# A two-layer hybrid trunk on one core: layer 0's lower convolutions and gates moved in the step order, and the mLSTM's key sums and squares rearranged

## The reference, cut to what matters

```python
# layer 0, recurrence
xc = causal_dwconv(xa, ...)                    # 4 taps, 8 tiles of 128 channels
r = sigmoid(block_diag(xc, wa) + ba)           # per tile: gates r and i
i = sigmoid(block_diag(xc, wx) + bx)
log_a = -8 * r * softplus(-lam)
b = sqrt(-expm1(2 * log_a)) * (i * xc)
h = scan(exp(log_a), b); ya = h * gelu(ga)
# layer 1, mLSTM, for each head
C_new = decay * C + sum_s kw_s v_s^T           # 512 x 512, for 8 samples and the prompt
n_new = decay * n + sum_s kw_s                 # the key sums
h = num / max(|den|, exp(-m))
h = h * rsqrt(mean(h * h) + eps)               # the mean of squares over a head's 512 rows
```

## Time and profile before

| | |
|---|---|
| median of three runs | 1156.18 us |
| the profiled execution's own time | 1151.86 us |
| its span in the trace | 1149.9 us |
| PE busy | 1084.2 us (94%) |
| DVE busy | 660.5 us (57%) |
| ACT busy | 543.3 us (47%) |
| GpSimd busy | 155.0 us (13%) |
| DMA | 260.97 MB, mean 227 GB/s |
| chain that ended last | PE 82%, DVE 10%, ACT 4%, DMA 2%, issue 1% |

### The profile page before, as it was taken

How to read it: one execution, slowest core, us unless ns; L and a number is a source line. 1 busy time by engine, 2 the same in 40 slices (tenths; PEclk the granted TensorE clock), 3 DMA queues, 4 the chain that set the end, 5 groups by cost and what they waited for, 6 DMA issues and landing times.

```text
span 1149.9 us, 21693 instructions
## 1 busy us (share of the span) xinstructions
PE 1084.2 (94%) x8497; PEld 949.2 (83%) x8497; DVE 660.5 (57%) x958; ACT 543.3 (47%) x885; POOL 155.0 (13%) x204
## 2 busy tenths in 40 slices
PE   4998999889999999999999999999999999999995
PEld 4987777668989999999999865555547989999995
DVE  4559584632376444335997546667686376544333
ACT  5332544532466553434575254554643456553431
POOL 5133000000104220001400410100000104220000
PEclk9998999899999999999999999999999999999998
DMA  9697797999534444443743039898999434444431
GB/s 337 229 331 273 275 378 289 351 346 385 170 115 167 165 163 166 166 164 126 271 151 129 22 105 389 308 393 297 395 340 398 166 127 165 165 164 165 166 128 41
DMA packets 92264, 260.97 MB, mean 227 GB/s; under 512 B 8836, under 2 KB 9860, under 8 KB 91800
## 3 DMA queue, kind: packets, MB, share of 16 engines
q1 hardware_dynamic: 91320, 257.92, 62.5%
q0 software_dynamic: 432, 1.29, 0.4%
q10 hardware_dynamic: 432, 0.65, 0.2%
HBM read 218.10 MB, written 41.73 MB: 226 GB/s over the span
## 4 chain that ended last, share of the span: by engine, by line
PE 82%; DVE 10%; ACT 4%; DMA 2%; issue 1%; SPq 0%; DVEq 0%; ACTq 0%
PE ps L2000 20%; PE ps L2001 19%; PE ps L2002 19%; PE ps L2484 2%; PE ps L2457 2%; PE ps L2112 2%; DVE w_lo L1200 2%; PE ps L2355 2%; PE ps L2193 1%; PE ps L2487 1%; PE ps L2399 1%; PE ps L2362 1%; DVE rstd L1230 1%; PE ps L2094 1%; PE ps L2064 1%
## 5 line engine op out<-in xcount | busy, mean ns | idle before, releaser
L1200 DVE TENSOR_TENSOR w_lo<-w_raw,w_hi 128x1024 fp32r<-128x1024 f32 x232 | 284.7, 1234 | 215.0 <-ACT w_hi L696 214.3
L696 ACT ACTIVATE w_hi<-w_raw 128x1024 fp32r<-128x1024 f32 x232 | 242.1, 1054 | 213.8 <-PE ps L2002 184.1
L2000 PE MATMUL ps<-xin_hi,w_hi 128*128 128x288 f32 x1016 | 307.8, 303 | 20.0 <-DVE w_lo L1200 19.9
L2001 PE MATMUL ps<-xin_lo,w_hi 128*128 128x288 f32 x1016 | 303.7, 299 | 0.0
L2002 PE MATMUL ps<-xin_hi,w_lo 128*128 128x288 f32 x1016 | 303.5, 299 | 0.0
L2000 PEld LDWEIGHTS ps<-xin_hi,w_hi 128*128 128x128 f32 x1016 | 194.7, 192 | 32.2 <-DVE w_lo L1200 21.1
L2001 PEld LDWEIGHTS ps<-xin_lo,w_hi 128*128 128x128 f32 x1016 | 193.6, 191 | 0.8 <-issue 0.2
L2002 PEld LDWEIGHTS ps<-xin_hi,w_lo 128*128 128x128 f32 x1016 | 193.4, 190 | 0.0
L2001 PE MATMUL ps<-hid_lo,w_hi 128*128 128x288 f32 x512 | 151.6, 296 | 0.0
L2002 PE MATMUL ps<-hid_hi,w_lo 128*128 128x288 f32 x512 | 151.3, 295 | 0.0
L2000 PE MATMUL ps<-hid_hi,w_hi 128*128 128x288 f32 x512 | 151.2, 295 | 0.0
(11 more groups left out here) (401 smaller groups left out, 1679.9 us busy)
## 6 DMA issues: line engine op xcount, KB each, us to landing
w_raw<-in_weights SPq DMA_DIRECT2D x232, 512.0 KB, 3.3
cring<-in_C SPq DMA_DIRECT2D x64, 512.0 KB, 6.3
out_Cs<-cring SPq DMA_DIRECT2D x64, 512.0 KB, 6.7
kv_a<-in_kv SPq DMA_DIRECT2D x52, 448.0 KB, 5.9
kv_b<-in_kv SPq DMA_DIRECT2D x52, 448.0 KB, 6.2
kv_w<-in_kv SPq DMA_DIRECT2D x24, 448.0 KB, 7.7
out_Cp<-cring SPq DMA_DIRECT2D x8, 512.0 KB, 5.9
x<-in_x SPq DMA_DIRECT2D x1, 1152.0 KB, 7.6
```

Of the source, the lines that this page charges most:

```text
L696: act.activation(w_hi[:, l % UM], w_raw[:, l % W_SLOTS], ACT.Copy).then_inc(hi_ready, 1)
L1200: dve.tensor_tensor(w_lo[:, l % W_SLOTS], w_raw[:, l % W_SLOTS], w_hi[:, l % UM], ALU.subtract).then_inc(lo_ready, 1)
L2000: pe.matmul(out, w_hi[:, j, ws], hi, start=start and kk == 0, stop=False)
L2001: pe.matmul(out, w_hi[:, j, ws], lo, start=False, stop=False)
```

## The change

In layer 0 the lower convolutions move from DVE's turns 18 to 21 to 22 to 25, the upper ones from 28, 30, 32, 33 to 30, 32, 34, 35. The gates are made in pairs, r and i of one tile together, on PE from step 23 (from 21 before) and on ACT from 25 (from 23 before). `decays(0)`, `input_roots(0)`, `input_scale(0)`, `recurrence(0)` and `gated(0)` come two turns later, `branch_gelu(0)` one later, `sample_scale(0)` two earlier. In the mLSTM the key sums swap operands: the selector (now padded to 128 columns) is the stationary operand and the keys the moving one, so the sums come out as rows, with n0 and its result laid out as rows too (`nrows`, one load and one more store). GpSimd adds the four squared tiles before one matmul of ones. The core of the diff:

```diff
-AB_USES = (["qs", "q0", "ks", "k0"] + [f"r{m}" for m in range(4)] + [f"i{m}" for m in range(4)]
-           + [f"r{m}" for m in range(4, 8)] + [f"i{m}" for m in range(4, 8)])
+AB_USES = ["qs", "q0", "ks", "k0"] + [f"{g}{m}" for m in range(MT) for g in "ri"]
...
# ACT, layer 0
-                if 23 <= g < 27:
-                    for m in range(2):
-                        gates((g - 23) // 2, 2 * ((g - 23) % 2) + m)
-                if g == 26:
-                    decays(0)
+                if 25 <= g < 25 + HM:
+                    gates(0, g - 25)
+                    gates(1, g - 25)
                 if g == 27:
                     sample_exp(0)
                 if g == 28:
+                    decays(0)
+                if g == 30:
                     input_roots(0)
-                if g == 30:
+                if g == 31:
                     branch_gelu(0)
...
# DVE, layer 0
-                if 18 <= g < 18 + HM:
-                    conv(g - 18)
+                if 22 <= g < 22 + HM:
+                    conv(g - 22)
...
-                if g == 27:
+                if g == 28:
+                    sample_scale(0)
+                if g == 29:
                     input_scale(0)
-                if g == 29:
+                if g == 31:
                     recurrence(0)
-                if g == 30:
-                    sample_scale(0)
-                if g == 31:
+                if g == 33:
                     gated(0)
-                if g in (28, 30, 32, 33):
-                    conv(HM + (28, 30, 32, 33).index(g))
+                if g in (30, 32, 34, 35):
+                    conv(HM + (30, 32, 34, 35).index(g))
...
# PE, layer 0
-                if 21 <= g < 25:
-                    for m in range(2):
-                        lru_gate((g - 21) // 2, 2 * ((g - 21) % 2) + m)
+                if 23 <= g < 23 + HM:
+                    lru_gate(0, g - 23)
+                    lru_gate(1, g - 23)
...
-                if 33 <= g < 37:
-                    for m in range(2):
-                        lru_gate((g - 33) // 2, HM + 2 * ((g - 33) % 2) + m)
+                if 33 <= g < 33 + HM:
+                    lru_gate(0, HM + g - 33)
+                    lru_gate(1, HM + g - 33)
...
# DVE, mLSTM
-                decay = bc[:, h % 2, R_DECAY:R_DECAY + NB]
-                pn = staged_v(h, "n")[:, 0:ET * (NB + 2)].rearrange("p (e b) -> p e b", b=NB + 2)
-                kn = pack_n[:, h * ET:(h + 1) * ET]
-                order.mark(dve.tensor_copy(kn[:, :, 0:1], pn[:, :, NB:NB + 1]))
-                order.after(dve.tensor_tensor(kn[:, :, 1:], n0_of(h).rearrange("p (e b) -> p e b", b=NB),
-                                              decay.unsqueeze(1).to_broadcast([P, ET, NB]), ALU.mult))
-                dve.tensor_tensor(kn[:, :, 1:], kn[:, :, 1:], pn[:, :, 0:NB], ALU.add).then_inc(stage_read_v, 1)
+                own = slice(N_S, N_S + NB)
+                pn = staged_v(h, "n")
+                if h == 0:
+                    dve.wait_ge(n0_in, 16)
+                dve.scalar_tensor_tensor(nrows[own, h], nrows[own, h], dcol[own, h:h + 1], pn[own], ALU.mult, ALU.add)
+                dve.tensor_copy(nrows[N_P:N_P + 1, h], pn[N_P:N_P + 1]).then_inc(stage_read_v, 1)
...
# GpSimd, mLSTM
-            for h in range(1, NH):
-                if h >= 2:
-                    pool.wait_ge(stage_full, use(h - 2, "vs") + 1)
-                head_diagonals(h)
+            def row_sums(h):
+
+                pool.wait_ge(h_sq, h + 1)
+                order.after(pool.tensor_tensor(qf[:, 0:2, 0:SEQ], qf[:, 0:2, 0:SEQ], qf[:, 2:4, 0:SEQ], ALU.add))
+                pool.tensor_tensor(qf[:, 0, 0:SEQ], qf[:, 0, 0:SEQ], qf[:, 1, 0:SEQ], ALU.add).then_inc(h_sum, 1)
+
+            for h in range(NH):
+                if h + 1 < NH:
+                    if h >= 1:
+                        pool.wait_ge(stage_full, use(h - 1, "vs") + 1)
+                    head_diagonals(h + 1)
+                row_sums(h)
...
# PE, mLSTM
-            def key_sums(h, tiles):
-
-                out = staged(h, "n") if 0 in tiles else ps[:, 6 + use(h, "n") % 2]
-                for e in tiles:
-                    c0 = (NB + 2) * e
-                    es = slice(P * e, P * e + P)
-                    for tt in range(2):
-                        pe.matmul(out[:, c0 + NB:c0 + NB + 1], ktok[:, tt, es], tokg[:, tt, NH + h:NH + h + 1],
-                                  start=tt == 0, stop=tt == 1)
-                    last = pe.matmul(out[:, c0:c0 + NB], kst[:, h % 2, es], seln, start=True, stop=True)
-                if ET - 1 in tiles:
-                    last.then_inc(stage_full, 1)
+            def key_sums(h):
+
+                out = staged(h, "n")
+                pe.matmul(out, seln, kst[:, h % 2], start=True, stop=False, skip_group_check=True)
+                for tt in range(2):
+                    last = pe.matmul(out[N_P:N_P + 1], tokg[:, tt, NH + h:NH + h + 1], ktok[:, tt],
+                                     start=False, stop=tt == 1, skip_group_check=True)
+                last.then_inc(stage_full, 1)
...
-                pe.wait_ge(h_sq, h + 1)
+                pe.wait_ge(h_sum, h + 1)
                 out = staged(h, "mean")
-                for e in range(ET):
-                    last = pe.matmul(out[:, 0:SEQ], ones, qf[:, e, 0:SEQ], start=e == 0, stop=e == ET - 1)
-                last.then_inc(stage_full, 1)
+                pe.matmul(out[:, 0:SEQ], ones, qf[:, 0, 0:SEQ], start=True, stop=True).then_inc(stage_full, 1)
...
                     if b == 1:
-                        key_sums(h, (0, 1))
+                        key_sums(h)
                     if b == 2:
                         row_squares(h)
                     if b in (3, 4):
                         outer(h, NB, b - 3)
                     outer(h, b, 0)
-                    if b == 1:
-                        key_sums(h, (2, 3))
```

More of the change, by code:

```diff
@@ L269, in program @@
         stri, o = at("stri", o, NS, parts=NS)
-        sel3, o = at("sel3", o, 2, NB, parts=3 * NS)
-        seln, o = at("seln", o, NB, dt=F32R, parts=3 * NS)
+        seln, _ = at("seln", o + 4 * NB, P, dt=F32R, parts=3 * NS)
+        sel3, o = at("sel3", o, NB + P, parts=3 * NS)
         gsml, o = at("gsml", o, 2 + NB, parts=NH)
@@ L468, in program @@
         h_sq = sem("h_sq")
+        h_sum = sem("h_sum")
+        n0_in = sem("n0_in")
         hs_psum = sem("hs_psum")
@@ L865, in _ @@
                     branch_gelu(1)
-                if 35 <= g < 39:
-                    for m in range(2):
-                        gates((g - 35) // 2, HM + 2 * ((g - 35) % 2) + m)
+                if 35 <= g < 35 + HM:
+                    gates(0, HM + g - 35)
+                    gates(1, HM + g - 35)
                 if g == 38:
@@ L1058, in _ @@
             act.activation(w3, ps[0:3 * NS, 5, 6 * NH:7 * NH], ACT.Copy, scale=DH ** -0.5)
-            act.activation(seln, sel3[:, 1], ACT.Copy).then_inc(gcol_taken, 1)
+            act.activation(dcol[N_S:N_S + NB], ps[N_S:N_S + NB, 5, 7 * NH:8 * NH], ACT.Copy)
+            act.activation(seln, sel3[:, NB:], ACT.Copy).then_inc(gcol_taken, 1)
             act.wait_ge(gcol_taken, 1)
@@ L1099, in own_values @@
                     act.wait_ge(c_mm, item(ho, bo, 1) + 1)
-                act.activation(vb[:, n % 2], vst[:, h % 2], ACT.Copy, scale=sel3[:, 0, b:b + 1]).then_inc(vb_ready, 1)
+                act.activation(vb[:, n % 2], vst[:, h % 2], ACT.Copy, scale=sel3[:, b:b + 1]).then_inc(vb_ready, 1)
             def sample_roots(c):
@@ L2324, in gate_columns @@
                 pe.transpose(ps[0:NS, 5, 5 * NH:6 * NH], rows[:, R_ENS:R_ENS + NS], four)
+                pe.matmul(ps[N_S:N_S + NB, 5, 7 * NH:8 * NH], rows[:, R_DECAY:R_DECAY + NB], four, start=True, stop=True,
+                          skip_group_check=True)
                 pe.transpose(ps[0:3 * NS, 5, 6 * NH:7 * NH], gw_c[:, SEQ:SEQ + 3 * NS], four).then_inc(gcol_ready, 1)
@@ L2617, in constants @@
     once = own3 * (np.arange(3 * NS) // NS != 1)[:, None]
-    c["sel3"] = np.concatenate([own3, once], 1)
+    c["sel3"] = np.concatenate([own3, np.pad(once, ((0, 0), (N_S, P - N_S - NB)))], 1)
     c["four_eyes"] = np.tile(np.eye(NS, dtype=f), (P // NS, 1))
@@ L2665, in lay_out @@
               "kv": np.concatenate([keys, vals]), "qkvw": np.concatenate(blocks, 1), "wgate": one(gate),
-              "gsml": small, "lru_wa": f["lru_wa"][0], "lru_wx": f["lru_wx"][0], "C0": f["state_mlstm_C"][0]}
+              "gsml": small, "n0rows": f["state_mlstm_n"][0].reshape(NB, NH * DH), "lru_wa": f["lru_wa"][0], "lru_wx": f["lru_wx"][0], "C0": f["state_mlstm_C"][0]}
     arrays.update(constants())
```

15 lines of the change are left out of this document (9 added, 6 removed).

## The result

| | before | after |
|---|---|---|
| median of six runs each | 1156.41 us (1150.87 to 1158.87) | 1144.53 us (1140.45 to 1145.81) |
| the profiled execution | 1151.86 us | 1144.92 us |
| its span | 1149.9 us | 1142.9 us |

The ratio is 0.9884, with a 95% interval of 0.9857 to 0.9911: between 10 and 17 us faster, 13.4 in the middle. The forecast was 8.7. The two profiled executions differ by 6.9 us only, the medians by 11.9.

The account below looks back on a forecast made before the run. PE was taken as the bound, busy 94% of the span. Layer 0's -6.7 and the mLSTM's -2.0 gave -8.7 us, 1143.2 from the profiled 1151.86, plus 4.3 for the median: 1147.5 us, range 1143.0 to 1154.0.

Parts of the forecast that it names:

- Layer 0, -6.7 us: Layer 0: later convolutions and gates remove PE's 4.24 us of idling and 2.5 us of slow clock, -6.7 us together.
- the stretch from 200 moves as a whole: Layer 0, 200 to 278 us: transfers wait for slots that PE frees, so the 6.7 us gained earlier is kept.
- What covers the moved work: Layer 0: DVE has 49 us of work in PE's 57; convolutions cost 2.1 us each, ACT's table loads nothing, DMA keeps up.
- Key sums, 0.2 us saved a head: mLSTM on PE: the new key sums take 1.94 us instead of 2.14 in each head.
- `new_n` 1.3 us, and PE's saving lost on DVE: mLSTM: `new_n` on DVE grows from 0.47 to 1.3 us, leaving 0.5 of PE's 1.4 us saving a head.
- GpSimd's sums: mLSTM: GpSimd's additions of squares end at 688.5, 0.3 us before PE arrives; on DVE they would be 4 x 0.7 us worse.
- the mLSTM's -2.0 us: mLSTM: 0.5 us gained in each head, -2.0 us in all, bounds +1 and -5.7.
- the median of the runs is 4.3 above that execution: Last step of the sum: 4.3 us added to 1143.2, the profiled execution's forecast, giving a median of 1147.5 us.
- The first: Rival, mLSTM: DVE has room, `new_n` costs little more, PE's full 5.7 us comes out; -12.4, 1143.8 us; chance 0.14.
- The other four: DMA holds layer 0, 1154.2 (0.10); sums block DVE updates, 1156.5 (0.03); DMA slows both, 1159.9 (0.05); half layer 0, 1150.9 (0.06).

## Why the prediction was right or wrong

- **Layer 0, -6.7 us: right, within what the runs can tell.** The idle time and the slow clock from 104 to 116 are gone, and the landmark at 204.28 had moved by 7.3, of which 0.36 came before the change's place. Alone the part measured 5.1 (mean span, interval 2.6 to 7.6). What I took for settled, that the stretch from 200 moves as a whole, held for the transfers: PE's wait for `kv_b` is 1.8 us, against 1.7. The clock there varies from one execution to the next: from 200 to 300 us it costs 6.9, 6.9 and 8.6 us in the three profiles of before, and 8.5, 5.2 and 6.8 in those of the whole change. So the 1.6 us more in the first profile of after tell nothing of the change.
- **What covers the moved work: right.** The convolution takes 1.70 us, the chain of the gates costs PE nothing, and nothing waits for keys. ACT's two added table loads show in no wait.
- **Key sums, 0.2 us saved a head: wrong by 0.3.** They take 2.25 us, 0.1 more than before; all of it was priced a little low, the first matmul at 0.3 for 0.44 us and the two fp32 ones at 1.64 for 1.81. What they are worth is their clock, some 6 us in all.
- **`new_n` 1.3 us, and PE's saving lost on DVE: right.** It takes 1.48 us, and the wait of 1.06 us is the 1.2 us that the squares save. The run with old squares starts the prompt's product at the same time, and the kernel with old key sums has a product 5.7 us lower.
- **GpSimd's sums: right.** They end 0.7 us early, the updates beside them take 1275 ns as before, and DVE in GpSimd's place costs 7 to 9 us.
- **The step that failed is the mLSTM's -2.0 us: measured -5.5.** It was added up from the work of PE and DVE alone, and the clock in the mLSTM was put at nothing, without a reason. The work gained nothing (product +0.4), so that even the -2.0 was too much, and the clock gave 5.8. That the edit of the key sums carries this clock is shown by the two kernels that undo half of the mLSTM part: 0.9798 with the old key sums, 0.9843 with the old squares.
- **The last step, "the median of the runs is 4.3 above that execution", has the same fault.** I added those 4.3 us to the result as if the change could not touch them. The profiled execution had a clock of 0.981, where the mean of before is 0.978: it had one half-clock spell behind the key sums, and the one profile of the longer group, to which 14 of 23 executions belong, has four. The sum, -8.7, and the measured difference of the two profiles, -6.9, are near each other; the median went further, because no execution of the whole change has so low a clock. What sets how many heads lose the clock in an execution is open.
- **Rivals.** The first gave 1143.8 us, next to the measured 1144.53, by a mechanism that did not happen: DVE has no room. To choose it would have been luck. The other four are refuted by full windows in 84 to 167 us, updates of 1275 ns and no wait for a loaded state. None of them was about the clock in the mLSTM, though the profile had the spell at 736 to 748.
